# A hybrid decoder step on one core: the rates and keys stage appended to the input projection's block, its row products taken one by one, and the group norm's units ordered by head pair

## The chip, the cores and the metric

The kernel runs on one core of one Trainium2 chip. The metric is the device time of one execution in microseconds (us). Below, PE is TensorE, ACT is ScalarE, DVE is VectorE, POOL is GpSimd, and SP is SyncE, which issues most of the transfers.

## The reference, cut to what matters

One layer, for 1024 prompt tokens and 8 sequences of 8 sample tokens that share all weights (1088 tokens, width 1024):

```
x += 1/2 gate1 * SwiGLU1(mod(RMSNorm(x)))            # d_ff 2816
P  = mod(RMSNorm(x)) @ w_in                          # 1792 RWKV columns, 768 attention columns
z  = u + (u_shift - u) * mu_shift                    # r, k, v, zw, za, zg
decay = exp(-exp(-softplus(-(w0 + tanh(zw) @ w2)) - 0.5))
a  = sigmoid(a0 + za @ a2)
kk = k * k_k;  kk = kk * rsqrt(max(sum_head(kk * kk), 1e-24))
k  = k * (1 + (a - 1) * k_a)
S  = S * decay + (S @ -kk) (kk * a)^T + v k^T;  o = S @ r          # per head of 64, per token
o  = group_norm_head(o) * ln_x_w + ln_x_b + sum_head(r * k * r_k) * v
x += gate2 * [o * (sigmoid(zg) @ g2), windowed attention] @ w_out
x += 1/2 gate3 * SwiGLU2(mod(RMSNorm(x)));  y = RMSNorm(x)
```

The changed stage computes everything from `decay` to the new `k`, in a scaled form: the running product of the decays within a chunk of 64 tokens is an exponential of a running sum, and a, b, k and r are multiplied by it or by its inverse.

## The kernel before

The stages follow one another: `ffn` (first), `input_projection`, `rwkv_keys`, `rwkv_heads`, `ffn` (second). Each is one `Block` with a program for each engine, and at the end of a block all engines meet. Tensors lie with features on the partitions and tokens along the free axis. The 512 RWKV features are `PAIRS` = 4 pairs of heads m; the tokens are cut into `UTILES` of 384, 384 and 320, called t here; a unit i is one (t, m), with t outermost, `NU` = 12 of them.

**Input projection.** 20 column groups (`WIN_ORDER`), each in three token tiles (`TILES`) of 368, 368 and 352. PE does 24 matmuls for each into banks 0 to 2; ACT takes the result out (`evac`, L1694), DVE adds the previous token's share (`add_previous`, L1812 to L1823), and counts each in `u_free`. Attention work (banks 3 to 7) lies between the products. The last column group has the sums of the keys' squares (bank 5), their root on ACT (L1780) and the reciprocal on DVE (L1891), which leaves `kk_rows`: 8 rows for each t, at partition 32t. After the last product, PE turns the last tokens' columns in bank 7 (L1673), ACT copies them out (L1797), and SP writes them to memory.

**Seam.** Then comes `k.release(...)` (L227): it clears semaphores and lets all engines meet a second time. `rwkv_keys` and `rwkv_heads` have only the end of a block between them.

**Rates and keys (`rwkv_keys`).** PE: for each unit, two products of 64 rows (`lora`, L1987: decay and a, in the two halves of the rows) into banks 0, 1 and 5 in turn; each has its own wait and its own increment. After each of the first four units, `back(m)` spreads the norms of pair m over the heads: three products of 8 rows (L1913, one for each t, in rows 0, 32 and 64) into banks 2 to 4, with one wait and one increment. Then `modulation(0)` (four products of `w_ada`, L275, each on a 1 MB slab that SP loads into one of three buffers once the product three before it has been done), the `bonus` products of the units (L2006), and between them the second modulation and two transposes (L283). ACT: the sigmoids (`rates`, L2030 and L2032), `key_factors(t)` for all four pairs at once (L2038) after unit 3 and after unit 11, then per unit two exponentials (L2048, L2049) and, six units behind, the copy of the bonus (L2069). DVE: `head_rk` (L2121), a copy of the scan's keep row into bank 7 (L2124), the keys (L2095), the running sums (L2102), and per unit four operations of `scale` (L2113 to L2118). POOL: per t, four products b (L2149), then per pair the new k and the bonus factor (L2153, L2155).

**Heads and group norm (`rwkv_heads`).** The recurrence in chunks; at its end the group norm over 12 units `FINISH` of (t, m), here with t outermost and tiles of 384, 384 and 256 tokens. In its last loop PE does, per unit, `back(i)` (L2606: 8 rows at partition 32t, spread over the heads) and `gate(i - 1)` (L2615: 128 rows), with the sample sequences' work in between (`sample_state(m)`: L2570, L2572, L2575). DVE scales unit i (L2816), then gates unit i-2 (L2822), POOL adds the bonus (L2394), and ACT and POOL split the result for the output projection, which begins the second `ffn` (L476 to L478). `gate(i)` waits until DVE has gated unit i-2.

Of the kernel before, what the change touches and what calls it, by code (L numbers as in the profile page):

```python
# [24 lines left out]
ALU = mybir.AluOpType  # L25
# [3 lines left out]
P = 128  # L29
# [1343 lines left out]
N_QKV = 6  # L1373

# [5 lines left out]
NK = WINDOW + TSEQ  # L1380


def input_projection(k):
# [33 lines left out]
    bank_s, bank_t, bank_o = k.psum[3:5], k.psum[5:7], k.psum[7]  # L1417
    LAST = 2 * NA + 2
# [39 lines left out]
    with k.nc.Block() as block:  # L1458
        @block.sync
        def _(sp):  # L1460
# [27 lines left out]
            for n in range(4, NC):  # L1488
# [4 lines left out]
                if n == 8:  # L1493
# [8 lines left out]
                    for s in range(NSEQ):  # L1502
# [10 lines left out]
            k.gates.load(sp, 6, 0, 0)  # L1513
            sp.wait_ge(last_done, 1)
# [3 lines left out]
                         ).then_inc(k.shift_out, 16)  # L1518

        @block.gpsimd  # L1520
        def _(pool):
            norm.odd_lows(pool, 2)
            for n in range(2, NC):
                win.low(pool, n)
                if n == 2:
                    pool.wait_ge(mm_done, at(0, NT - 1))
                    for j in range(2):
                        pool.memset(rot[j][:], 0.0).then_inc(zeroed, 1)
                if n == N_QKV + 2:
                    pool.wait_ge(roped, 5)  # L1530
                    pool.tensor_copy(q_new[:].rearrange("p s (c t) -> p s c t", t=TSEQ),
                                     k.qkv[:, 0:4, NP_TOK:T].rearrange("p c (s t) -> p s c t", t=TSEQ)).then_inc(q_done, 1)

        @block.tensor
        def _(pe):
# [118 lines left out]

            def previous():
                pe.wait_ge(shift_in, 16)
                pe.transpose(k.psum[7][:, 0:NR], k.shift_rows[0:NR, :], k.c("ident")[0:NR, 0:NR]).then_inc(prev_mm, 1)
# [13 lines left out]
            pe.wait_ge(z_done, UC)  # L1671
            pe.wait_ge(o_done, NA)
            pe.transpose(k.psum[7][0:9 * UC, 0:P], k.last[:].rearrange("p s c -> p (s c)"), k.c("ident")).then_inc(last_mm, 1)  # L1673

        @block.scalar
        def _(act):
# [79 lines left out]
            def attention(s):  # L1756
# [21 lines left out]
                if s == LAST + 3:  # L1778
                    act.wait_ge(ss_done, 1)
                    act.activation(k.kk_rows[0:72, :], k.kk_rows[0:72, :], ACT.Sqrt).then_inc(root_done, 1)  # L1780

# [13 lines left out]
            act.activation(k.es[0], k.es[0], ACT.Sigmoid)  # L1795
            act.wait_ge(last_mm, 1)
            act.copy(k.last_rows[0:9 * UC, :], k.psum[7][0:9 * UC, 0:P]).then_inc(last_done, 1)  # L1797

        @block.vector
        def _(dve):  # L1800
# [78 lines left out]
            for n in range(NC):  # L1879
                if n >= N_QKV:  # L1880
                    for t in range(NT):
# [7 lines left out]
                        if s == LAST + 4:  # L1889
                            dve.wait_ge(root_done, 1)  # L1890
                            dve.reciprocal(k.kk_rows[0:72, :], k.kk_rows[0:72, :])  # L1891
# [4 lines left out]


UNITS = [(t, m) for t in range(len(UTILES)) for m in range(PAIRS)]
NU = len(UNITS)


def sums_to_rows(k, pe, bank, m, sq):

    for t, (a, n) in enumerate(UTILES):
        ins = pe.matmul(bank[32 * t:32 * t + 8, 0:n], k.c("to_rows")[:, 8 * m:8 * m + 8], sq[:, a:a + n],
                        start=(m == 0), stop=(m == PAIRS - 1))
    return ins


def row_to_heads(k, pe, out, m, t, rows):  # L1910

    r, n = slice(32 * t, 32 * t + 8), UTILES[t][1]
    return pe.matmul(out[:, 0:n], k.c("from_rows")[r, P * m:P * m + P], rows[r, 0:n], start=True, stop=True)  # L1913


def rows_to_heads(k, pe, banks, m, rows):

    for t in range(len(UTILES)):
        ins = row_to_heads(k, pe, banks[t], m, t, rows)
    return ins  # L1920


def rwkv_keys(k):

    d = k.dram
    C = float(np.exp(-0.5))
    k.bb = k.at("bb", R1_AT + PAIRS * TB, [P, PAIRS, T])  # L1930
    k.bon = k.at("bon", R1_AT, [P, PAIRS, T])
    log_d = k.at("log_d", R1_AT + 3 * PAIRS * TB, [P, PAIRS, T])
    keep, w2a2, ada = k.keep, k.w2a2, k.gates
    head_rk = k.at("head_rk", R2_AT + TB + 4 * RW, [P, PAIRS, P])
    turned = k.psum[5][:, 0:256]
    lora_mm, rates_done, back_mm, kk_done, kf_done = (
        k.sem(f"pr_{n}") for n in ("lora_mm", "rates_done", "back_mm", "kk_done", "kf_done"))
    sum_done, exp_done, b_done, bonus_in, bonus_mm, bonus_done, scaled = (
        k.sem(f"pr_{n}") for n in ("sum_done", "exp_done", "b_done", "bonus_in", "bonus_mm", "bonus_done", "scaled"))
    rk_done = k.sem("pr_rk_done")  # L1940

    KEEP_FROM = NP_TOK - TW_U
    KEEP0 = [0 if a < UTILES[-1][0] else a - KEEP_FROM for a, n in UTILES]
    NT_U = len(UTILES)

    def cut(tensor, m, t):
        a, n = UTILES[t]
        return tensor[:, m, a:a + n]

    def spans(t):  # L1950

        a, n = UTILES[t]
        out = [(0, min(a + n, NP_TOK) - a, HD)]
        if a + n > NP_TOK:
            out.append((NP_TOK - a, n, TSEQ))
        return out

    def lora_bank(n):
        return k.psum[(0, 1, 5)[n % 3]]

    def inv_bank(i):
        return k.psum[2 + i % 2][:, 0:UTILES[UNITS[i][0]][1]]

    def prd_bank(i):
        return k.psum[4 if i % 2 == 0 else 7][:, 0:UTILES[UNITS[i][0]][1]]

    def bonus_bank(i):
        return k.psum[i % 2][:, 0:UTILES[UNITS[i][0]][1]]

    with k.nc.Block() as block:  # L1970
        @block.sync
        def _(sp):
            for s in range(1, 8):
                if s >= 3:
                    sp.wait_ge(ada.used, s - 2)
                ada.load(sp, 6 + s // 4, s % 4, s % 3)
            sp.wait_ge(k.shift_out, 32)

        @block.tensor
        def _(pe):  # L1980
            def lora(i):
                t, m = UNITS[i]
                a, n = UTILES[t]
                for h, r in enumerate(HALVES):
                    if 2 * i + h >= 3:
                        pe.wait_ge(rates_done, 2 * i + h - 2)
                    pe.matmul(lora_bank(2 * i + h)[:, 0:n], w2a2[r, P * m:P * m + P], k.u[r, 12, a:a + n], start=True, stop=True  # L1987
                              ).then_inc(lora_mm, 1)

            def modulation(n):  # L1990
                if n:
                    pe.wait_ge(ada.rows, n)
                for s in range(4 * n, 4 * n + 4):
                    ada.product(pe, s % 4, s % 3, s // 3 + 1)
# [6 lines left out]
            def bonus(i):  # L2001
                t, m = UNITS[i]
                pe.wait_ge(bonus_in, i + 1)
                if i >= 2:
                    pe.wait_ge(bonus_done, i - 1)
                pe.matmul(bonus_bank(i), head_rk[:, m], cut(k.bon, m, t), start=True, stop=True).then_inc(bonus_mm, 1)  # L2006

            pe.wait_ge(k.lora_in, 32)
            for i in range(NU):
                lora(i)  # L2010
                if i < PAIRS:
                    back(i)
            pe.wait_ge(rates_done, 2 * NU)
            modulation(0)
            pe.wait_ge(rk_done, 1)
            for i in range(NU):
                bonus(i)
                if i == 1:
                    ada.turn(pe, 0, turned)
                    modulation(1)  # L2020
                if i == 7:
                    ada.turn(pe, 1, turned)

        @block.scalar
        def _(act):
            def rates(i):
                t, m = UNITS[i]
                n = UTILES[t][1]
                act.wait_ge(lora_mm, 2 * i + 1)
                act.activation(cut(log_d, m, t), lora_bank(2 * i)[:, 0:n], ACT.Sigmoid, bias=k.p2("rwkv_w0", m)).then_inc(rates_done, 1)  # L2030
                act.wait_ge(lora_mm, 2 * i + 2)
                act.activation(cut(k.bb, m, t), lora_bank(2 * i + 1)[:, 0:n], ACT.Sigmoid, bias=k.p2("rwkv_a0", m)  # L2032
                               ).then_inc(rates_done, 1)

            def key_factors(t):
                act.wait_ge(rates_done, 2 * PAIRS * (t + 1))
                for m in range(PAIRS):
                    act.activation(cut(k.bon, m, t), cut(k.bb, m, t), ACT.Identity, scale=k.p2("rwkv_k_a", m),  # L2038
                                   bias=k.one_ka[:, m:m + 1]).then_inc(kf_done, 1)

            def exps(i):
                t, m = UNITS[i]
                act.wait_ge(sum_done, NU if i == 1 else i + 1)
                if i >= 2:
                    act.wait_ge(scaled, i - 1)
                else:
                    act.wait_ge(kk_done, NU)
# [1038 lines left out]
```

## Time and profile before

| | |
|---|---|
| three runs | 2457.2, 2460.49, 2455.1 us; median 2457.2 |
| profiled execution | 2462.48 us, of which the span of the trace is 2460.4 |
| granted TensorE clock, mean | 0.978 |
| PE busy | 2367.4 us, 96% of the span |
| DVE, POOL, ACT busy | 1104.2, 537.9, 387.5 us |
| rates and keys | 1194.7 to 1251.5 us |
| group norm's last loop | 1498.9 to 1539.9 us |

Times of rows are in us from the start of the span. A timeline row has a start, a length, the engine, the line, the operation, its shapes and the number of instructions merged in it; a bracket tells how long the engine stood idle before it and what released it. An fp32 product is two MATMUL instructions. A granted clock of 1.00 is 2.4 GHz and 0.50 is 1.2 GHz.

### The profile page before, as it was taken

How to read it: one execution, taken by the hardware profiler on the slowest of the kernel's cores; microseconds unless marked ns; L12 is line 12 of the kernel's file. 1: busy time of each engine (PE TensorE's matmuls, PEld its weight loads, DVE VectorE, ACT ScalarE, POOL GpSimd, SP SyncE). 2: the span in 40 equal slices, each digit the busy share in tenths (PEclk: the TensorE clock that was granted, in tenths of full speed). 3: DMA queues.
4: the chain of work that ended last, by engine and by line, in shares of the span. 5: the costliest groups of instructions: out<-in, count | busy, mean ns of one | idle time of the engine just before them, and what ended most of it. 6: DMA issues, size and time to landing. Idle time of an engine off the chain costs nothing. (4 is left out here: it accounts for less than half of the span.)

```text
span 2460.4 us, 50589 instructions
## 1 busy us (share of the span) xinstructions
PE 2367.4 (96%) x21666; PEld 2247.0 (91%) x21666; DVE 1104.2 (45%) x2446; ACT 387.5 (16%) x890; POOL 537.9 (22%) x278
## 2 busy tenths in 40 slices
PE   5999999999999999999889899999999999999997
PEld 4999999999999989888468885999999999999997
DVE  4524443334444364434577664147334444433344
ACT  4100000000000232434521122131000000000003
POOL 2312121212212032111332133413212112121111
PEclk8999999999999999999799998999999999999999
DMA  9232221111011142100220002332111011111101
GB/s 338 86 103 84 87 86 52 50 36 51 17 51 51 49 111 59 35 26 30 98 66 5 4 13 63 107 103 69 45 41 50 18 51 51 51 51 34 51 9 73
DMA packets 160634, 151.22 MB, mean 61 GB/s; under 512 B 21488, under 2 KB 141985, under 8 KB 160088
## 3 DMA queue, kind: packets, MB, share of 16 engines
q1 hardware_dynamic: 159960, 146.75, 19.0%
q8 instruction: 119, 1.95, 0.3%
q10 hardware_dynamic: 144, 2.23, 0.2%
q14 instruction: 27, 0.22, 0.0%
q0 software_dynamic: 384, 0.07, 0.0%
HBM read 137.98 MB, written 11.34 MB: 61 GB/s over the span
## 5 line engine op out<-in xcount | busy, mean ns | idle before, releaser
L476 PE MATMUL bank<-hh,f_up_hi 128*128 128x368 f32 (+1 forms) x2112 | 693.4, 328 | 11.4 <-ACT hh L416 9.5
L478 PE MATMUL bank<-hh,f_up_lo 128*128 128x368 f32 (+1 forms) x2112 | 690.9, 327 | 0.0
L477 PE MATMUL bank<-hl,f_up_hi 128*128 128x368 f32 (+1 forms) x2112 | 690.2, 327 | 0.0
L1189 DVE TENSOR_TENSOR f_prod<-f_silu,bank 128x368 f32<-128x368 f32 x132 | 70.2, 532 | 767.4 <-PE bank L478 767.3
L476 PEld LDWEIGHTS bank<-hh,f_up_hi 128*128 128x128 f32 x2112 | 396.8, 188 | 17.7 <-issue 17.6
L477 PEld LDWEIGHTS bank<-hl,f_up_hi 128*128 128x128 f32 x2112 | 397.0, 188 | 0.0
L478 PEld LDWEIGHTS bank<-hh,f_up_lo 128*128 128x128 f32 x2112 | 396.9, 188 | 0.0
L491 DVE SCALAR_TENSOR_TENSOR x<-bank,mods,x 128x368 f32<-128x368 f32 (+1 forms) x544 | 306.2, 573 | 200.3 <-PE bank L478 188.1
L944 POOL TENSOR_TENSOR f_up_lo<-f_up_raw,f_up_hi 128x2048 fp32r<-128x2048 f32 x44 | 203.3, 4620 | 778.1 <-DVE f_up_hi L1176 778.1
L476 PE MATMUL bank<-f_a_hi,f_dn_hi 128*128 128x368 f32 (+1 forms) x1056 | 346.6, 328 | 0.8 <-DVE f_scratch L494 0.8
L478 PE MATMUL bank<-f_a_hi,f_dn_lo 128*128 128x368 f32 (+1 forms) x1056 | 345.3, 327 | 0.0
L477 PE MATMUL bank<-f_a_lo,f_dn_hi 128*128 128x368 f32 (+1 forms) x1056 | 344.8, 327 | 0.0
L1127 ACT ACTIVATE f_silu<-bank 128x368 f32<-128x368 f32 x132 | 62.4, 473 | 1442.1 <-PE bank L478 1442.1
L476 PEld LDWEIGHTS bank<-f_a_hi,f_dn_hi 128*128 128x128 f32 x1056 | 198.2, 188 | 1.7 <-DVE f_scratch L494 1.3
L477 PEld LDWEIGHTS bank<-f_a_lo,f_dn_hi 128*128 128x128 f32 x1056 | 198.3, 188 | 0.0
L478 PEld LDWEIGHTS bank<-f_a_hi,f_dn_lo 128*128 128x128 f32 x1056 | 198.2, 188 | 0.0
L949 POOL TENSOR_TENSOR f_dn_lo<-f_dn_raw,f_dn_hi 128x2048 fp32r<-128x2048 f32 x22 | 102.3, 4650 | 383.3 <-DVE f_dn_hi L1182 383.3
L476 PE MATMUL bank<-hh,w_in_hi 128*128 128x368 f32 (+1 forms) x480 | 163.7, 341 | 2.2 <-POOL hl L408 2.2
L477 PE MATMUL bank<-hl,w_in_hi 128*128 128x368 f32 (+1 forms) x480 | 159.1, 331 | 0.0
L478 PE MATMUL bank<-hh,w_in_lo 128*128 128x368 f32 (+1 forms) x480 | 158.9, 331 | 0.0
L476 PEld LDWEIGHTS bank<-hh,w_in_hi 128*128 128x128 f32 x480 | 91.9, 192 | 15.0 <-issue 14.7
L1362 POOL TENSOR_TENSOR w_in_lo<-w_in_raw,w_in_hi 128x1024 fp32r<-128x1024 f32 x18 | 47.1, 2614 | 223.0 <-DVE w_in_hi L1357 223.0
(377 smaller groups left out, 2814.7 us busy)
## 6 DMA issues: line engine op xcount, KB each, us to landing
f_up_raw<-in_ffn_w_gu SPq DMA_DIRECT2D x88, 512.0 KB, 5.0
f_dn_raw<-in_ffn_w_down SPq DMA_DIRECT2D x22, 1024.0 KB, 7.6
ada<-in_w_ada SPq DMA_DIRECT2D x12, 1024.0 KB, 16.2
late<-in_w_ada SPq DMA_DIRECT2D x12, 1024.0 KB, 4.9
w_in_raw<-in_w_in SPq DMA_DIRECT2D x16, 512.0 KB
gates<-in_w_ada SPq DMA_DIRECT2D x8, 1024.0 KB, 6.4
x_in<-in_x_prompt SPq DMA_DIRECT2D x8, 512.0 KB, 8.5
gate<-in_w_ada SPq DMA_DIRECT2D x4, 1024.0 KB, 5.1
```

What stands on the lines that cost most here:

```text
L476: pe.matmul(out, wh, rh, start=(n == 0), stop=False)
L477: pe.matmul(out, wh, rl, start=False, stop=False)
L478: ins = pe.matmul(out, wl, rh, start=False, stop=(n == last))
L491: ins = dve.scalar_tensor_tensor(x[:, a:a + np_], bank[:, 0:np_], gate[:, 0:1], x[:, a:a + np_], ALU.mult, ALU.add)
L944: pool.tensor_tensor(up_lo[j][:], up_raw[:], up_hi[j][:].bitcast(F32), ALU.subtract).then_inc(up_lo_done, 1)
L949: pool.tensor_tensor(dn_lo[:], dn_raw[:], dn_hi[:].bitcast(F32), ALU.subtract).then_inc(dn_lo_done, 1)
L1127: act.activation(silu[u % 2][:, 0:n], k.psum[2 * (u % 2)][:, 0:n], ACT.Silu).then_inc(gate_free, 1)
L1189: dve.tensor_tensor(prod[u % 2][:, 0:n], silu[u % 2][:, 0:n], k.psum[2 * (u % 2) + 1][:, 0:n], ALU.mult).then_inc(up_free, 1)
L1362: pool.tensor_tensor(lo[:], self.raw_of(n)[:], hi[:].bitcast(F32), ALU.subtract).then_inc(self.lo_done, 1)
```

## The change

`rwkv_keys` is no longer a block. It returns five functions, one for each engine, that `input_projection` calls at the end of its own programs, so that each engine goes on without meeting the others. What the meeting gave is now written as waits: `lora` waits for `u_free` (called `u_last`) and, for bank 5, for `ss_done`; the row products wait for the last `u_free`, for `max_done`, `t_done` and for a new semaphore `kk_ready` behind the reciprocal; DVE waits for `o_done` before it writes bank 7, for `win.lo_done` before `head_rk`; the modulation waits for `last_done`, as does the bonus.

- `back(m)` with three row products becomes twelve `back(q)`, each with its own wait and increment, through banks 2, 3, 4 and 6; they stand after units 1 to 5 in groups of 3, 2, 3, 2 and 2.
- `key_factors` is spread: from unit 4 on, ACT does one key factor after each unit's rates. The factors of the third t stay where they were.
- The transpose of the last tokens moves behind unit 7 and to bank 6; the sigmoid that brings in ACT's table moves up behind the root (L1780).
- DVE does all twelve keys before the first running sum, and `head_rk` after the last.
- SP issues the slabs 1 and 2 of the first modulation when the last product is done, ahead of the last tokens' transfers.
- `k.release` stands between this joint block and `rwkv_heads`.
- `FINISH` is ordered by pair: (0,3), (1,3), (0,2), (1,2), ... for the first eight units; the third t is as before. PE's last loop takes two units at a time: `back(2j)`, `back(2j+1)`, `gate(2j-1)`, `gate(2j)`.

```diff
+    BACK_BANKS = (2, 3, 4, 6)
+    BACK_AT = {1: (0, 1, 2), 2: (3, 4), 3: (5, 6, 7), 4: (8, 9), 5: (10, 11)}
...
-                    if 2 * i + h >= 3:
-                        pe.wait_ge(rates_done, 2 * i + h - 2)
+                n_before = 2 * i + h
+                if n_before >= 3:
+                    pe.wait_ge(rates_done, n_before - 2)
+                elif n_before == 2:
+                    pe.wait_ge(ss_done, 1)
+                else:
+                    pe.wait_ge(u_last, U_SLOTS - 2 + n_before)
...
-            def back(m):
-                if m >= 1:
-                    pe.wait_ge(kk_done, NT_U * m)
-                rows_to_heads(k, pe, k.psum[2:5], m, k.kk_rows).then_inc(back_mm, 1)
+        def back(q):
+            if q == 0:
+                pe.wait_ge(u_last, U_SLOTS)
+                pe.wait_ge(max_done, NA)
+                pe.wait_ge(kk_ready, 1)
+            elif q == 3:
+                pe.wait_ge(t_done, 2 * NA)
+            elif q >= len(BACK_BANKS):
+                pe.wait_ge(kk_done, q + 1 - len(BACK_BANKS))
+            m, t = divmod(q, NT_U)
+            row_to_heads(k, pe, back_bank(q), m, t, k.kk_rows).then_inc(back_mm, 1)
...
             for i in range(NU):
                 lora(i)
-                if i < PAIRS:
-                    back(i)
+            for q in BACK_AT.get(i, ()):
+                back(q)
+            if i == PAIRS + 3:
+                pe.wait_ge(kk_done, NU)
+                turn_last(pe)
...
             for i in range(PAIRS):
                 rates(i)
-            key_factors(0)
             for i in range(PAIRS, NU):
                 rates(i)
-            key_factors(1)
+            key_factors(i // PAIRS - 1, (i % PAIRS,))
+            if i == PAIRS + 4:
+                copy_last(act)
...
-FINISH = [(t, m) for t in range(3) for m in reversed(range(PAIRS))]
+FINISH = [(t, m) for m in reversed(range(PAIRS)) for t in range(2)] + [(2, m) for m in reversed(range(PAIRS))]
...
-            for i in range(FSAMPLE):
-                back(i)
-                if i >= 1:
-                    gate(i - 1)
+            for j in range(FSAMPLE // 2):
+                back(2 * j)
+                back(2 * j + 1)
+                if j:
+                    gate(2 * j - 1)
+                gate(2 * j)
...
         input_projection(k)
-        k.release(keep=(k.cache_out, k.shift_out, k.lora_in, k.keep_in, *k.gates.sems))
-        rwkv_keys(k)
+        k.release(keep=(k.cache_out,))
         rwkv_heads(k)
```

## Rows read from the trace of the kernel before

**Rows 1.** The page: busy time of each engine, share of the span, instructions.
```profile
PE 2367.4 (96%) x21666; PEld 2247.0 (91%) x21666; DVE 1104.2 (45%) x2446; ACT 387.5 (16%) x890; POOL 537.9 (22%) x278
```

**Rows 2.** Busy time by stretch: PE, PEld, DVE, ACT, POOL, clock, DMA share, GB/s.
```profile
1190.00:1252.00 62.00, 46.17 (x245) 21.01 (x249) 42.17 (x90) 38.91 (x87) 33.92 (x38) 0.72 0.34 120
1252.00:1456.00 204.00, 181.53 (x7005) 173.62 (x6996) 142.92 (x334) 28.73 (x62) 31.94 (x40) 1.00 0.05 11
1456.00:1542.00 86.00, 82.44 (x1092) 50.03 (x1087) 41.61 (x69) 28.49 (x54) 43.27 (x46) 0.85 0.18 53
```

**Rows 3.** Timeline of PE, from the last input product to the heads.
```profile
1189.39 0.32 PE L478 MATMUL bank<-hh,w_in_lo 128*128 128x352 f32 x1
...
1194.74 1.65 PE L1987 MATMUL bank<-au,w2a 64*128 64x384 f32 x4 [2.92 <-PEq L230]
1196.32 1.65 PE L1913 MATMUL bank<-kk_rows,const 8*128 8x384 f32 x6
1197.90 1.65 PE L1987 MATMUL bank<-au,w2a 64*128 64x384 f32 x4
...
1208.01 11.31 PE L1987 MATMUL bank<-au,w2a 64*128 64x384 f32 x32
1219.94 2.80 PE L275 MATMUL bank<-gates,cT 128*32 128x256 f32 x48 [0.62 <-ACT bb L2032]
...
1239.73 1.36 PE L275 MATMUL bank<-gates,cT 128*32 128x256 f32 x16 [2.65 <-DMA gates<-in_w_ada]
1241.03 4.45 PE L2006 MATMUL bank<-bon,head_rk 128*128 128x384 f32 x8
...
1251.58 0.33 PE L2234 MATMUL bank<-au,bb 64*64 64x128 f32 x2 [0.77 <-PEq L1970]
```

**Rows 4.** Timeline of ACT in the same stretch.
```profile
1191.85 0.27 ACT L1797 COPY last_rows<-bank 126x128 f32<-126x128 f32 x1
1196.40 0.58 ACT L2030 ACTIVATE log_d<-bank,par 128x384 f32<-128x384 f32 x1 [4.28 <-PE bank L1987]
1196.87 0.57 ACT L2032 ACTIVATE bb<-bank,par 128x384 f32<-128x384 f32 x1
...
1207.40 2.50 ACT L2038 ACTIVATE bon<-bb,rest,par 128x384 f32<-128x384 f32 x4
...
1250.85 0.42 ACT L2069 COPY bon<-bank 128x320 f32<-128x320 f32 x1 [0.21 <-PE bank L2006]
```

**Rows 5.** Timeline of DVE in the same stretch.
```profile
1190.89 0.27 DVE L1816 SCALAR_TENSOR_TENSOR au<-bank,par,au 128x56 f32<-128x56 f32 x1
...
1224.53 0.55 DVE L2113 SCALAR_TENSOR_TENSOR au<-au,bank 128x378 f32<-128x378 f32 x1 [4.37 <-POOL bb L2149]
...
1249.51 0.23 DVE L307 SCALAR_TENSOR_TENSOR mods<-mods,par 128x72 f32<-128x72 f32 x1
```

**Rows 6.** Timeline of POOL in the same stretch.
```profile
1208.28 3.87 POOL L2149 TENSOR_TENSOR bb<-bb,au 128x384 f32<-128x384 f32 x4 [43.59 <-ACT bon L2038]
...
1242.71 0.86 POOL L2155 TENSOR_TENSOR bon<-au 128x320 f32<-128x320 f32 x1
```

**Rows 7.** Two single microseconds around the rise of the clock, columns as in rows 2.
```profile
1215.00:1216.00 1.00, 1.00 (x4) 0.95 (x4) 0.96 (x1) 0.99 (x2) 0.86 (x2) 0.50 0.00 0
...
1217.00:1218.00 1.00, 0.98 (x6) 0.66 (x5) 0.51 (x1) 0.94 (x4) 0.86 (x2) 1.00 0.00 0
```

**Rows 8.** Timeline of PE in the group norm's last loop.
```profile
1498.92 1.64 PE L2606 MATMUL bank<-gn_rows,const 8*128 8x384 f32 x2
...
1512.03 0.91 PE L2615 MATMUL bank<-au,g 128*128 128x384 f32 x2
1512.88 0.91 PE L2606 MATMUL bank<-gn_rows,const 8*128 8x384 f32 x2
```

**Rows 9.** Timeline of DVE in the same loop.
```profile
1512.14 0.61 DVE L2816 SCALAR_TENSOR_TENSOR au<-au,par,bank 128x384 f32<-128x384 f32 x1 [3.40 <-PE bank L2606]
1512.67 0.55 DVE L2822 TENSOR_TENSOR au<-au,bank 128x384 f32<-128x384 f32 x1
```

More of the change, by code:

```diff
@@ L1380, with sums_to_rows, row_to_heads @@
 NK = WINDOW + TSEQ
+UNITS = [(t, m) for t in range(len(UTILES)) for m in range(PAIRS)]
+NU = len(UNITS)
+def sums_to_rows(k, pe, bank, m, sq):
+    for t, (a, n) in enumerate(UTILES):
+        ins = pe.matmul(bank[32 * t:32 * t + 8, 0:n], k.c("to_rows")[:, 8 * m:8 * m + 8], sq[:, a:a + n],
+                        start=(m == 0), stop=(m == PAIRS - 1))
+    return ins
+def row_to_heads(k, pe, out, m, t, rows):
+    r, n = slice(32 * t, 32 * t + 8), UTILES[t][1]
+    return pe.matmul(out[:, 0:n], k.c("from_rows")[r, P * m:P * m + P], rows[r, 0:n], start=True, stop=True)
@@ L1417, in input_projection @@
     bank_s, bank_t, bank_o = k.psum[3:5], k.psum[5:7], k.psum[7]
+    kk_ready = k.sem("kk_ready")
+    keys = rwkv_keys(k, win, u_free, max_done, ss_done, t_done, o_done, kk_ready, last_done)
+    keys_sync, keys_tensor, keys_scalar, keys_vector, keys_gpsimd = keys
     LAST = 2 * NA + 2
@@ L1513, in _ @@
             k.gates.load(sp, 6, 0, 0)
+            sp.wait_ge(mm_done, at(NC - 1, NT - 1))
+            k.gates.load(sp, 6, 1, 1)
+            k.gates.load(sp, 6, 2, 2)
             sp.wait_ge(last_done, 1)
@@ L1653, in attention, with turn_last @@
                         key_sums(2 * (s - LAST - 1) + m)
+            def turn_last(pe):
+                pe.wait_ge(z_done, UC)
+                pe.wait_ge(t_done, 2 * NA)
+                pe.transpose(bank_t[1][0:9 * UC, 0:P], k.last[:].rearrange("p s c -> p (s c)"), k.c("ident")).then_inc(last_mm, 1)
             def previous():
@@ L1670, in _ @@
                         attention(slot(n, t))
-            pe.wait_ge(z_done, UC)
-            pe.wait_ge(o_done, NA)
-            pe.transpose(k.psum[7][0:9 * UC, 0:P], k.last[:].rearrange("p s c -> p (s c)"), k.c("ident")).then_inc(last_mm, 1)
+            keys_tensor(pe, turn_last)
         @block.scalar
@@ L1780, in attention, with copy_last @@
                     act.activation(k.kk_rows[0:72, :], k.kk_rows[0:72, :], ACT.Sqrt).then_inc(root_done, 1)
+                    act.activation(k.es[0], k.es[0], ACT.Sigmoid)
+            def copy_last(act):
+                act.wait_ge(last_mm, 1)
+                act.copy(k.last_rows[0:9 * UC, :], bank_t[1][0:9 * UC, 0:P]).then_inc(last_done, 1)
             norm.roots(act, 2)
@@ L1794, in _ @@
                         attention(slot(n, t))
-            act.activation(k.es[0], k.es[0], ACT.Sigmoid)
-            act.wait_ge(last_mm, 1)
-            act.copy(k.last_rows[0:9 * UC, :], k.psum[7][0:9 * UC, 0:P]).then_inc(last_done, 1)
+            keys_scalar(act, copy_last)
         @block.vector
@@ L1895, in _ @@
                     rope(n - 1)
[L1898 to L1913, printed above, removed]
@@ L2729, in _ @@
             sample_o_end()
[L2730 to L2734 removed]
+            for j in range(FSAMPLE // 2):
[4 more added lines that the diff above has]
+                gate(2 * j)
+                if j == 0:
                     sample_mean()
[L2736 removed]
+                if j == 2:
                     sample_sums()
[L2738 removed]
+                if j == 3:
                     sample_back()
[L2740 to L2741 removed]
+                if j < PAIRS:
+                    sample_state(j)
             gate(FSAMPLE - 1)
```

401 lines of the change are left out of this document (200 added, 201 removed).

## The prediction

> **What bounds the kernel now.** The page's first part comes first: PE is busy 2367.4 of 2460.4 us, and no other engine reaches half [rows 1]. So the time is PE's, and a change can win only where PE is not doing full work. The busy time by stretch shows where that is: from 1190 to 1252 us PE is busy 46.2 of 62 us and at a mean clock of 0.72, so both idle and slow; in the group norm's stretch it is busy nearly always, but at 0.85 [rows 2]. These are the two places that the diff touches. Nothing else in PE's order changes, so what either stage saves or costs moves all that follows it, one for one.
>
> In the first place the timelines are read engine by engine. PE's last input product ends at 1189.71, its first rates product starts at 1194.74, the last ends at 1219.32, and the heads start at 1251.58 [rows 3]. Which chain ties 1219.32 to 1251.58? PE starts the modulation at 1219.94; its slabs are loaded one after another, each into a buffer that an earlier product must have left, and the last of the eight arrives at 1239.73, where PE had waited for the transfer. Behind that product in PE's order stand ten of the twelve bonus products, which start at 1241.03, alternate with ACT's exponentials and end with ACT's copy at 1251.27 [rows 3, 4]. DVE is done at 1249.74, POOL at 1243.57 [rows 5, 6]. So the end of the stage hangs on the start of the modulation, and that on the end of the rates products.
>
> **Part 1, the seam in front.** The products for unit 0 and the first of unit 1 need no result of the last tile, so PE goes on at 1189.71 in place of 1194.74. The second of unit 1 needs the first rate from ACT. ACT is free at about 1190.4, since its table load has moved up; that load, 1.3 us by the idle stretch it then fills behind the root, lies in front of the evacuation of the last group's second tile, which only feeds DVE, and DVE's reciprocal ends as ACT takes out the third tile: I cost it at nothing, and at 1.3 us if DVE turns out late. With a rate of 0.58 [rows 4] this product starts at 1191.1. The first three row products need DVE's last add, which ends at 1191.16 [rows 5]. Together they end at about 1192.4 (lower bound 1191.9, if they run alone at full clock; upper 1193.0, if they fall to the half clock).
>
> **Part 2, rates and row products.** Before, the stretch from 1194.74 to 1219.32 held twelve pairs of rates products and four groups of row products. A pair and a group take 1.58 each at the half clock of that stretch (1196.32 - 1194.74, 1197.90 - 1196.32) [rows 3]. One row product alone takes 1.57 at that clock too (1.64 with its tail), and three in one group 1.65 [rows 3, 8]: products in different rows run side by side, and a group costs what one of them costs. Do they still when each has its own wait and increment? The trace shows no single row products with waits of their own, but it shows the pairs of rates products, which have them and still take 1.65 for two. So I take five groups at 1.58, one of them already counted in part 1. The bounds: 0 more if all share, and 7 x 1.57 = 11.0 us more if none of the seven that ride along does. Their waits for DVE (a bank is free after the key four products before it) are one or two groups old when PE comes to them. What is left after 1192.4 is ten pairs and four groups: 24.58 - 2 x 1.58 = 21.4 us, and 0.4 for the transpose that has moved in: 1214.2. That is 5.1 us earlier than 1219.32.
>
> The Trainium skill ("TensorE: Matmul & The Clock Gate", section "The cost: per-tile semaphore tail") says that increments of packed products queue up at some 26 ns each. By it, an estimate, twelve increments in place of four add 8 x 26 ns = 0.2 us; the sum does without it.
>
> **Part 3, what follows from it.** ACT now does eight key factors between the rates: 0.62 each (2.50 / 4) beside 0.94 for a unit's two rates (2 x 0.47) [rows 4], so 1.56 a unit, as much as PE's pair at half clock: just covered, and it is what would bind if PE were faster. POOL begins its stream when the fourth factor is there. Before, it ran without a pause from 1208.28 to 1243.57 [rows 6]. After, the fourth factor comes with unit 7 at about 1209.3, when three of the four b are done, so POOL is only 1.9 us ahead and ends at 1241.7: still before the end of the chain. DVE's twelve keys, twelve sums and `head_rk` are done by about 1217.4, and the scales, which took 25.2 us with their waits (1224.53 to 1249.74) [rows 5], end before 1245. So the chain of slabs stays the last, 5.1 us earlier: ACT's last copy at 1246.2. The two slabs that SP now issues at 1189.7 were never the late ones (they have until 1214); I cost that at nothing, with or without it. The last tokens' transfers move behind ACT's copy at unit 8, hidden under 30 us of the stage. **Stage: -5.1.**
>
> **Part 4, the release moves back.** From ACT's copy (end 1192.12) to PE's start at 1194.74 the release and the two meetings take 2.6 us; from ACT's last copy (1251.27) to the heads at 1251.58 one meeting takes 0.3 [rows 3, 4]. The release now stands at the second place, the cheap meeting at the first is gone. The 2.6 contains SP's two last transfers (about 0.8), which won't be there. So +1.5, between +1.2 and +2.3.
>
> **Part 5, the group norm.** In PE's last loop a row product takes 0.84 and a gate 0.85 at full clock (1512.03 to 1512.88 and on) [rows 8], and PE never waits. The first eight units now alternate between rows 0 and 32, so two row products run for the price of one: 4 x 0.84 = 3.4 us. But `gate(2j)` now needs DVE's gating of unit 2j-2, which stands behind the scaling of unit 2j: 0.61 + 0.55 less overlap, and about 0.1 for each handover, 1.25 us after the row product [rows 9]; PE has only `gate(2j-1)`, 0.85, to do meanwhile. Three times about 0.35, so -3.4 + 1.1 = **-2.3**. Who waits behind that gate is `sample_state`, and nobody else. The last four units share the same rows and gain nothing. The sums of the early units run side by side too, but they wait for ACT's squares: nothing. Bounds: -3.4, and 0 if the slower part of the clock (0.50 in the rows at 1498.92 [rows 8]) grows by as much as is saved.
>
> **The sum.** -5.1 + 1.5 - 2.3 = -5.9. On the profiled execution's own 2462.5 us that is 2456.6. That execution lies 5.3 above the median of 2457.2; the same difference on the median gives **2451.3**.
>
> **The rivals.**
> *The clock stays full in the rates.* Before, the clock was still 0.50 at 1215 and 1.00 only at 1217, with PE busy all the time since 1194.74 [rows 3, 7]; ahead of that the engine had been idle for most of 5 us. After, that gap is below 1 us. If the clock stays at 2.4 GHz, ACT binds: from 1190.4, eight units at 0.94, four at 0.84, eight factors at 0.62 and a copy, 16.1 us, to 1206.5; the modulation starts 13.2 us earlier, its chain ends at 1238.1, after POOL (about 1234) and DVE (about 1236). The sum is -13.2 + 1.5 - 2.3 = -14.0: 2443.2. Against it: in the rates of before, PE was never idle and stayed at 1.2 GHz for over 20 us with products of 64 and of 8 rows; they don't seem to count as full work. The Trainium skill, "TensorE: Matmul & The Clock Gate" (Part 1), holds that the array is slow by default and sustained matmul activity gives it the full clock; by that rule PE, never idle for long now, would be at full clock here. The trace agrees only in part, with 0.50 at 1215 under a PE that is busy all the time [rows 7]. Chance 0.17.
> *The loop of the group norm gives nothing.* The clock there falls and rises with the mix of products, and two products at once leave PE more idle rows or more waits; -5.1 + 1.5 = -3.6: 2453.6. Chance 0.22.
> *The heads start at half clock.* The release leaves PE idle for nearly 2 us right before the heads, after a thin stretch, where before it was 0.8. Heads are 89% PE [rows 2]; each microsecond at 1.2 GHz costs up to 0.5. Below 12 us it only eats the gain, 2457 at most; from about 22 us on the kernel is slower by more than 0.2%. Against it: at 1.00 these products held the full clock for 204 us. Chance 0.07.
> *The single row products don't overlap.* Then part 2 costs 11.0 more and the group norm gives nothing and adds no wait: -5.1 + 11.0 + 1.5 = +7.4: 2464.6, slower. It decides from the fourth of the seven on (4 x 1.57 > 5.9), and shows as slower by 0.2% only with all seven. Against it: the pairs of rates products. Chance 0.06.
>
> **How the numbers follow.** The likeliest case has what is left, 0.48, with a range of its own from -9.5 to -2.5 (the clock rising earlier or later by one change, the bounds of parts 1, 4 and 5). All cases together: 2443 holds the full-clock case, 2458.5 all but the last. What a measurement of this kernel tells from no change is about 0.2%, or 4.9 us. Below 2452.3 lie two thirds of the likeliest case, nearly all of the full-clock one and a fifth of the third: 0.32 + 0.16 + 0.05 = 0.53. Above 2462.1: the last rival and a rest of the fourth, 0.08. Between, 0.39.
>
> **What would show it.** PE's first rates product right after the last input product, with no gap of 5 us; rates products ending near 1214; L275 starting then, and its last slab near 1234.6; the heads' first product near 1248; groups of row products with 1.6 us for two or three; in the last loop pairs of 384-column row products at about 0.9 us for two. The prediction is wrong if the clock in the rates is 1.00, if the row products stand in line, if POOL's or DVE's stream and not the slabs ends the stage, or if the heads begin at 0.50.

## The result and the profile after

The changed kernel takes **2446.6 us** (median of 7 runs, 2442.4 to 2449.5) against 2457.2 for the kernel before (7 runs on the same chip). The ratio is 0.995, with an interval of [0.9939, 0.9961], so it saves between 9.6 and 15.0 us; the ratio itself stands for 12.3, and the medians differ by 10.6. The forecast was 2451.3, a gain of 5.9. The direction was right. The mechanism named for the first place was wrong in its clock: what came there was the rival to which the forecast gave 0.17. The profiled execution took 2446.64 us, with a span of 2444.9. It lies on the median, whereas the profiled execution of before lay 5.3 above its own.

The page's busy line, against [rows 1]: PE is busy for 15.8 us less, with the same 21666 instructions. So the products themselves became shorter, not only the gaps between them.

```profile
PE 2351.6 (96%) x21666; PEld 2237.9 (92%) x21666; DVE 1105.4 (45%) x2446; ACT 386.2 (16%) x890; POOL 537.1 (22%) x278
```

Busy time by stretch, columns as in [rows 2]. The first stretch is 10 us shorter, and its mean clock is 0.90 where it was 0.72. The heads are unchanged.

```profile
1190.00:1242.00 52.00, 38.05 (x225) 15.70 (x223) 43.37 (x90) 36.23 (x82) 33.56 (x36) 0.90 0.39 143
1242.00:1446.00 204.00, 181.90 (x7015) 174.00 (x7016) 143.21 (x334) 28.74 (x62) 32.55 (x41) 1.00 0.05 11
1446.00:1530.00 84.00, 76.61 (x1095) 49.32 (x1092) 41.00 (x69) 28.82 (x55) 44.28 (x47) 0.88 0.21 60
```

Timeline of PE from the last input product to the heads, against [rows 3]:

```profile
1188.78 0.32 PE L478 MATMUL bank<-hh,w_in_lo 128*128 128x352 f32 x1
1189.03 2.49 PE L1480 MATMUL bank<-au,w2a 64*128 64x384 f32 x8
1191.44 0.91 PE L1399 MATMUL bank<-kk_rows,const 8*128 8x384 f32 x6
1192.29 0.92 PE L1480 MATMUL bank<-au,w2a 64*128 64x384 f32 x4
1193.13 0.91 PE L1399 MATMUL bank<-kk_rows,const 8*128 8x384 f32 x4
...
1206.68 0.80 PE L1480 MATMUL bank<-au,w2a 64*128 64x320 f32 x2 [0.21 <-ACT log_d L1534]
1208.52 2.80 PE L275 MATMUL bank<-gates,cT 128*32 128x256 f32 x48 [1.04 <-ACT bb L1536]
...
1228.14 1.94 PE L275 MATMUL bank<-gates,cT 128*32 128x256 f32 x16 [3.38 <-DMA gates<-in_w_ada]
1230.01 4.50 PE L1508 MATMUL bank<-bon,head_rk 128*128 128x384 f32 x8
...
1242.08 0.33 PE L2271 MATMUL bank<-au,bb 64*64 64x128 f32 x2 [2.29 <-PEq L230]
```

There is no gap at 1189, and a pair of rates products or a group of row products takes 0.85 from start to start, where before it took 1.58. That is the full clock, as the window over the middle of them shows (columns as in [rows 2]):

```profile
1198.00:1202.00 4.00, 3.97 (x16) 1.68 (x15) 3.28 (x6) 3.92 (x9) 2.18 (x3) 1.00 0.00 0
```

The rates products end at 1207.48, the modulation starts at 1208.52 (before: 1219.94) and the heads start at 1242.08 (before: 1251.58). The last input product ends at 1189.10, before at 1189.71, so 0.6 us of each of these differences was gained ahead of the changed stage.

Timelines of ACT, DVE and POOL in the same stretch, against [rows 4 to 6]:

```profile
1184.63 1.28 ACT L2074 ACT_TABLE_LOAD   x1
...
1197.57 0.70 ACT L1542 ACTIVATE bon<-bb,rest,par 128x384 f32<-128x384 f32 x1
...
1239.83 0.43 ACT L1573 COPY bon<-bank 128x320 f32<-128x320 f32 x1 [0.21 <-PE bank L1508]
```

```profile
1209.80 3.04 DVE L1635 TENSOR_SCALAR head_rk<-const,par 128x128 f32<-128x128 f32 x4
1212.76 0.54 DVE L1618 SCALAR_TENSOR_TENSOR au<-au,bank 128x378 f32<-128x378 f32 x1
...
1238.49 0.23 DVE L307 SCALAR_TENSOR_TENSOR mods<-mods,par 128x72 f32<-128x72 f32 x1
```

```profile
1198.44 1.00 POOL L1654 TENSOR_TENSOR bb<-bb,au 128x384 f32<-128x384 f32 x1 [34.36 <-DVE au L1600]
...
1234.77 0.87 POOL L1660 TENSOR_TENSOR bon<-au 128x320 f32<-128x320 f32 x1
```

ACT's last copy ends the stage at 1240.26, DVE is done at 1238.72 and POOL at 1235.64. The slabs' chain still binds, and the release behind it takes 1.8 us, as forecast.

Timeline of PE in the group norm's last loop, against [rows 8]:

```profile
1495.24 0.91 PE L2643 MATMUL bank<-gn_rows,const 8*128 8x384 f32 x4
1496.09 0.91 PE L2652 MATMUL bank<-au,g 128*128 128x384 f32 x2
1497.32 0.91 PE L2652 MATMUL bank<-au,g 128*128 128x384 f32 x2 [0.32 <-DVE au L2861]
```

Two row products run in 0.85. Of the two gates behind them, the second waits 0.32 for DVE's gating. The same wait comes three times (1497.32, 1503.04, 1509.30).

### The profile page after: what moved, and what is told of

It is laid out like the page before. It is cut to its first block and busy times, and to the rows that moved or that the text cites. A ratio compares the mean times of both kernels' runs of the same rounds, so it can differ in the third digit from the quotient of the medians.

```text
span 2444.9 us, 50581 instructions
## 1 busy us (share of the span) xinstructions
PE 2351.6 (96%) x21666; PEld 2237.9 (92%) x21666; DVE 1105.4 (45%) x2446; ACT 386.2 (16%) x890; POOL 537.1 (22%) x278
## 3 DMA queue, kind: packets, MB, share of 16 engines
q1 hardware_dynamic: 159960, 146.75, 19.1%
## 5 line engine op out<-in xcount | busy, mean ns | idle before, releaser
L476 PE MATMUL bank<-hh,f_up_hi 128*128 128x368 f32 (+1 forms) x2112 | 693.3, 328 | 11.8 <-ACT hh L416 9.5
```

What stands on the lines that cost most here:

```text
L476: pe.matmul(out, wh, rh, start=(n == 0), stop=False)
```

## The experiments

All medians stand beside the kernel before on the same chip. A gain in us that stands behind a ratio is worked out from that ratio; it can differ from the difference of the two medians by one or two us. The two parts of the change were first taken alone.

**The stage alone.** The changed kernel with the group norm of before:

```diff
-FINISH = [(t, m) for m in reversed(range(PAIRS)) for t in range(2)] + [(2, m) for m in reversed(range(PAIRS))]
+FINISH = [(t, m) for t in range(3) for m in reversed(range(PAIRS))]
...
-            for j in range(FSAMPLE // 2):
-                back(2 * j)
-                back(2 * j + 1)
-                if j:
-                    gate(2 * j - 1)
-                gate(2 * j)
+            for i in range(FSAMPLE):
+                back(i)
+                if i >= 1:
+                    gate(i - 1)
```

> The joint block alone, group norm in the old order. My reading of the trace after: the seam and the rates hold most of the gain, because PE no longer idles before the rates and they run at 2.4 GHz. Expected -8 us against before (about 2449), with L1480-type rates products ending within 19 us of the last input product and a clock of 1.00 there. Rival: the clock has nothing to do with it and the append brings only what was forecast, -3.6 us (2453.6).

Measured: 2449.4 against 2459.8, ratio 0.9964 [0.9951, 0.9977], or -8.9 us. In its trace the rates products end 18.4 us after the last input product, as in the changed kernel. The expectation of -8 us held.

**The group norm alone.** The same edit the other way round, on the kernel before.

> The group norm's order alone, on the kernel before. Expected -2.5 us (2454.7): four pairs of row products that share their time, less three waits of 0.3 us, plus 1 us in the sums. The forecast had -2.3. Rival: it gives as much as the trace after shows between the row products and the output projection (-5), then it would be 2452.

Measured: 2452.8, ratio 0.9971 [0.9959, 0.9983], or -7.1 us. That is three times my -2.3. The two parts alone add up to -16.0, more than the -12.3 of the whole. The intervals are wide enough to allow that; the runs are repeated below.

**The gap in front of the rates.** Is it the idle stretch that decides the clock? The first kernel is the changed one with nine ACT copies ahead of the first rate, and PE's first rates product waits for them. The second kernel has the same copies and the same wait, but PE does seven products (fourteen passes) of 128 rows in the time in which it would stand idle.

```diff
+            pe.wait_ge(held, 1)
...
+        for j in range(9):
+            ins = act.copy(k.bon[:, j % 4, 352 * (j // 4):352 * (j // 4) + 352], k.u[:, 4, 0:352])
+        ins.then_inc(held, 1)
```

```diff
+            pe.wait_ge(u_last, U_SLOTS - 2)
+            pe.wait_ge(max_done, NA)
+            for _ in range(7):
+                pe.matmul(k.psum[3][:, 0:384], k.c("ident"), k.u[:, 12, 0:384], start=True, stop=True)
```

> The kernel after, but ACT does nine more copies (352 columns each, about 3.9 us) before its first rate, and PE stands idle until they are done; no result is changed. If an idle stretch before the rates is what puts PE at 1.2 GHz for the whole of them, the clock is 0.50 there and the time is up by 4 + about 7 us (2457). If the mix of products sets the clock and not the idle stretch, the clock stays 1.00 and the time is up by 4 us (2450.6).

> The same as gap_idle, with seven products of 128 rows and 384 columns on PE in the time in which it stood idle there (results not used). Both theories: the clock stays 1.00 and the time is up by 4 us against after (2450.6). If it falls to 0.50 here as well, the delay itself and not the idle PE matters, for example the place of the rates in time.

Measured: 2461.0 with the idle gap, ratio 1.0006 [0.9997, 1.0015], and 2453.2 with the filled one, ratio 0.997 [0.9958, 0.9982]. PE's timeline of the kernel with the idle gap, and the window over its rates:

```profile
1188.28 0.32 PE L478 MATMUL bank<-hh,w_in_lo 128*128 128x352 f32 x1
1192.82 3.96 PE L1481 MATMUL bank<-au,w2a 64*128 64x384 f32 x8 [4.22 <-ACT bon L1578]
1196.70 1.65 PE L1399 MATMUL bank<-kk_rows,const 8*128 8x384 f32 x6
...
1215.22 6.54 PE L1481 MATMUL bank<-au,w2a 64*128 64x320 f32 x16
```

```profile
1193.00:1221.00 28.00, 28.00 (x72) 11.40 (x73) 15.37 (x23) 15.15 (x30) 7.42 (x8) 0.50 0.10 40
```

And PE's timeline of the kernel with the filled gap:

```profile
1190.40 4.68 PE L1514 MATMUL bank<-au,const 128*128 128x384 f32 x14
1195.01 2.49 PE L1481 MATMUL bank<-au,w2a 64*128 64x384 f32 x8
1197.43 0.92 PE L1399 MATMUL bank<-kk_rows,const 8*128 8x384 f32 x6
```

PE comes to its first rates product equally late in both, 4.2 and 4.5 us after the last input product. But after 4.22 us of idling it runs 28 us at a clock of 0.50, though never idle, and after products it runs at full clock. From first to last, the rates products take 28.9 us in the one (1192.82 to 1221.76) and 19.1 in the other (1195.01 to 1214.10). The medians differ by 7.8 us, as expected, and every run shows the difference: the mean granted clock of a whole execution is 0.978 to 0.981 in all eleven runs with the idle gap and 0.982 to 0.986 in all six with the filled one. So the rates run slowly after an idle stretch of this size and fast when full-height products stand in its place. Whether any work would do in its place, or only products of 128 rows, was not separated.

**The gap filled in the kernel before.** If the gap is all that matters, filling products should do in the kernel before what the joined block does. Three of them stand ahead of the wait for DVE's last add and two behind the transpose.

```diff
+            pe.wait_ge(max_done, NA)
+            for _ in range(3):
+                pe.matmul(k.psum[3][:, 0:384], k.c("ident"), k.u[:, 12, 0:384], start=True, stop=True)
...
+            for _ in range(2):
+                pe.matmul(k.psum[3][:, 0:384], k.c("ident"), k.u[:, 12, 0:384], start=True, stop=True)
```

> The kernel before, with three products of 128 rows and 384 columns on PE ahead of its wait for the last tile and two behind the transpose (results not used), so that PE idles about 1.7 us in one piece ahead of the rates and not 1.8 and 2.9. If the idle stretch alone is what put the rates at 1.2 GHz, they run at 2.4 GHz now and are bound by ACT: about -7 us against before (2452), as much as the append gained beyond its forecast and more. If it needs the append as well (rates that follow the products without a pause), nothing changes, or it is up by the 0.3 us by which PE may come late to the meeting.

Measured: 2454.1 against 2455.6, ratio 0.9993 [0.9984, 1.0002]. A miss. PE's timeline and windows:

```profile
1195.12 0.92 PE L1992 MATMUL bank<-au,w2a 64*128 64x384 f32 x4 [1.70 <-PEq L230]
1195.97 0.91 PE L1918 MATMUL bank<-kk_rows,const 8*128 8x384 f32 x6
1196.81 1.54 PE L1992 MATMUL bank<-au,w2a 64*128 64x384 f32 x4
1198.60 1.65 PE L1918 MATMUL bank<-kk_rows,const 8*128 8x384 f32 x6 [0.25 <-DVE au L2100]
```

```profile
1197.00:1211.00 14.00, 13.48 (x41) 5.26 (x40) 11.16 (x18) 7.36 (x15) 3.81 (x4) 0.51 0.34 136
1211.00:1218.00 7.00, 6.36 (x35) 3.36 (x36) 5.59 (x7) 6.94 (x15) 6.57 (x8) 1.00 0.00 0
```

The rates begin at full clock; the clock falls at 1197 and rises again at 1211. The rates end 26.7 us after the last input product, where before it was 29.6. The wait for the last slab takes most of that back: its product starts at 1239.06, 0.7 earlier than in [rows 3]. The 1.70 us of the release was left idle here. In the joined block, which has no such gap, the clock stayed full. That this rest of a gap is the reason is not shown: one execution without any gap, below, also lost the clock.

**Key factors, and two ways of ending the stage sooner.** There are three variants of the changed kernel. One has the key factors in groups of four again. One has the first three slab products moved up behind the last three units of rates. The third has, on top of that, `head_rk` computed in DVE's wait ahead of the keys.

```diff
+        key_factors(0)
...
-            key_factors(i // PAIRS - 1, (i % PAIRS,))
...
+        key_factors(1)
```

```diff
+            if i >= NU - 3:
+                early(i - NU + 3)
```

> The kernel after, with the key factors of the first t in one piece behind unit 3 and those of the second behind unit 11, as before. The slabs of the modulation end the stage in the trace after, so the order of the factors should be worth nothing either way: within 1 us of after (2446.6). Rival: POOL or ACT binds and the spread was worth something; then it is 2 us or more slower.

> The kernel after, with the first three products of the modulation behind units 9, 10 and 11 in place of behind all rates, so that their buffers come free about 2.5 us earlier. If only the transfers set the end of the stage, it ends up to 2.5 us earlier (2444). If the fifth product's wait for DVE (its rows are copied behind the third scale) sets when the last slab is asked for, it gives about nothing, or costs up to 1 us where the products stand in ACT's way.

> early_slabs, and DVE makes head_rk while it waits for the first row products, where POOL is idle. In after it took 3.04 us there against 0.87 before. Expected: 0.87 again, the scales 1.5 to 2 us earlier, and with both waits eased the stage ends 2 to 3 us earlier than in after (2444). Rival: the copy of the rows is not late for any slab, and the end moves by less than 1 us.

Measured, against 2455.6: 2446.9 with the factors grouped, ratio 0.9961 [0.9949, 0.9974]; 2443.3 with early slabs, 0.9952 [0.9939, 0.9966]; 2443.2 with `head_rk` as well, 0.9953 [0.994, 0.9966]. What spreading the factors is worth can't be told from these medians. The trace of the kernel with grouped factors showed something else. PE's timeline, and the window behind it:

```profile
1193.08 0.92 PE L1480 MATMUL bank<-au,w2a 64*128 64x384 f32 x4
1193.92 1.12 PE L1399 MATMUL bank<-kk_rows,const 8*128 8x384 f32 x4
1194.98 1.65 PE L1480 MATMUL bank<-au,w2a 64*128 64x384 f32 x4
```

```profile
1196.00:1215.00 19.00, 18.70 (x49) 7.87 (x47) 13.02 (x20) 11.38 (x23) 11.70 (x12) 0.50 0.04 14
```

There is no gap ahead of the rates, and yet the clock falls inside the row products at 1194.7. The edit can't be the cause: ACT does its first key factor at 1197.60, and up to the fall this kernel and the changed one do the same. In this execution the rates end 24.8 us after the last input product and the heads start 59.1 after it, close to my likeliest case. So the joined block allows the full clock; it does not guarantee it. Of the eight profiled executions with the joined block and no added gap this is the only one. The runs without a profile hint at a few more: the stage alone had one of 2457.8 us in the first set and one of 2459.0 in the repeat, both with a mean clock of 0.979, where its others show 0.981 to 0.986. The mean of a whole execution doesn't tell where the clock was low, so this stays a hint.

With early slabs the last slab's product starts at 1225.94 (in the changed kernel at 1228.14), which is 2.3 us earlier when counted from the last input product. Timelines of PE without and with the moved `head_rk`:

```profile
1235.35 2.77 PE L1512 MATMUL bank<-bon,head_rk 128*128 128x320 f32 x8
1240.41 0.33 PE L2277 MATMUL bank<-au,bb 64*64 64x128 f32 x2 [2.29 <-PEq L230]
```

```profile
1235.62 4.27 PE L1512 MATMUL bank<-bon,head_rk 128*128 128x320 f32 x8
1242.18 0.33 PE L2277 MATMUL bank<-au,bb 64*64 64x128 f32 x2 [2.29 <-PEq L230]
```

The second comes to its last slab 0.9 us sooner (1225.02), but 0.7 of that lies ahead of the stage, so the moved `head_rk` brings 0.2 there. It then starts the heads 2.4 us later, counted from the last input product. Of this 1.5 us is that the last eight passes run at half clock (4.27 in place of 2.77). The rest lies between the last slab and these passes.

**The same again, on one chip.** To see whether the parts add, and whether the clock repeats, three of these kernels and the changed one were run side by side.

> The changed kernel once more, as the yardstick of the other three on the same chip. It stood 10.6 us below the kernel before (0.995). If the full clock in the joint block is what the block gives whenever nothing empties TensorE's queue, the rates' products end some 18 to 19 us after the last input product again. If it is a matter of chance from one execution to the next, as the one execution with grouped key factors suggests, some profiled executions of these four kernels show it at half by 1196, and the rates end 7 us later in them.

> The appended stage alone, with the group norm as before. Alone it stood 8.9 us below the kernel before, the group norm alone 7.1 us, both together 10.6 us: these don't add up. Theory A, the two parts are additive and the earlier two medians were each a few us off: here the appended stage gives 6 to 8 us and the difference to the changed kernel is 3 to 5 us. Theory B, the group norm's part is worth less behind the appended stage: 9 us again, and a difference of under 2.5 us.

> The group norm's order alone, on the kernel before. Theory A (additive): 3 to 5 us below the kernel before. Theory B (worth more by itself than behind the appended stage): 7 us again. My forecast of this part was 2.3 us, which would be a ratio of 0.9991.

> The changed kernel with the first three modulation products issued after the last three rate units. In its profiled execution the heads began 1.7 us earlier than in the changed kernel's. If that is the kernel's and not the execution's, its median stands 1.5 to 3.5 us below that of the changed kernel on this chip; if not, within 1 us.

Measured, against 2460.8:

| kernel | median us | ratio, interval |
|---|---|---|
| changed kernel | 2449.8 | 0.9952 [0.9936, 0.9967] |
| stage alone | 2451.8 | 0.9964 [0.9953, 0.9974] |
| group norm alone | 2455.7 | 0.9982 [0.9971, 0.9992] |
| early slabs | 2448.3 | 0.9958 [0.9941, 0.9976] |

The changed kernel repeats, and so does the stage alone. So the stage alone came as theory B had it (-8.9 again, and 2.0 between its median and that of the changed kernel), and the group norm alone as theory A had it (-4.4). The two alone now sum to -13.3 against -11.8 for both together, so they add up within the intervals. The intervals of the group norm's -7.1 and -4.4 overlap, and neither is shown to be off. How much the group norm is worth behind the new stage these medians don't settle. They don't tell early slabs from the changed kernel either.

The traces say more, since each profiled execution can be cut at the same instructions. All times are in us: from the last input product's end to the last rates product's end, to the heads' start, and from the first row product of the last loop to the first output product.

| kernel (one execution) | rates end | heads start | last loop |
|---|---|---|---|
| before | 29.6 | 61.9 | 43.1 |
| before, fillers | 26.7 | 61.5 | 41.0 |
| group norm alone, twice | 29.6; 29.6 | 65.5; 62.7 | 40.5; 37.1 |
| stage alone, twice | 18.4; 19.0 | 52.8; 53.8 | 40.7; 40.1 |
| changed, twice | 18.4; 18.4 | 53.0; 54.5 | 39.0; 36.9 |
| factors grouped | 24.8 | 59.1 | 36.9 |
| early slabs, twice | 19.3; 19.3 | 51.2; 51.2 | 37.0; 36.8 |
| early slabs, `head_rk` | 19.3 | 53.7 | 36.9 |
| idle gap; filled gap | 33.2; 23.5 | 67.6; 57.4 | 36.9; 40.6 |

The mean of the stage is 63.4 in the three executions with the old stage and no filler, and 53.5 in the four with the new stage: -9.8. Four executions of the old loop average 41.2 and ten of the new one 37.9: -3.4. Together that is -13.2, inside the interval of the ratio. The stretch between the two, in which only the order of the sums differs, varies by itself: from the heads' start to the last loop it takes 243.7 to 250.4 us over all fourteen. So does the old stage, with 61.9, 65.5 and 62.7 us in three executions, though their rates end at the same 29.6.

## Why the forecast was half right

The direction and the nearness of 2451.3 owe something to luck: most of the gain came for a reason that the forecast held unlikely, and the time that it gave to that rival, 2443.2, lies nearer to the measured 2446.6. The forecast's likeliest case had a range of its own from -9.5 to -2.5, and the measured -10.6 to -12.3 lies outside it. That the measured time lies inside the whole range, from 2443 to 2458.5, is due to the full-clock rival that the range had to hold. The forecast itself had called a clock of 1.00 in the rates a sign of being wrong.

**Part 1** held. PE goes on behind the last input product, and the first group of row products ends at 1192.35, by the forecast at 1192.4. Counted from the last input product that is 3.3 us against 2.7, at the upper bound; the times of 1192.35 and 1192.4 agree because the last input product ended 0.6 earlier here.

**Part 2 failed in its premise.** It priced a group at 1.58, the half clock that [rows 3] show, and set the end at 1214.2, 24.5 us after the last input product's end. The count was right: groups of two or three row products with waits of their own still cost one. The price was 0.85, and the rates ended 18.4 us after the last input product. I had seen that PE ran without a pause for 20 us at the half clock before and concluded that such thin products hold it there. The kernels with the idle and the filled gap show the other reading: in these two the products kept the clock that they found, for most of the block. Before, they found the half clock, after nearly 5 us with little to do. What makes the chip grant one level or the other stays open: the fillers in the kernel before, and the grouped-factors execution, lost the full clock under the same kinds of product. The full clock was the first rival, at 0.17. Its sum of -13.2 for the stage was 2.4 to 2.8 too large: counted from the last input product, the modulation starts 10.8 earlier and ACT's last copy ends 10.4 earlier. ACT doesn't bind from the start: up to unit 4 it still waits 0.64 to 1.10 for PE, and only from unit 6 on are the units 1.4 to 1.6 apart. The grouped-factors execution shows that the premise could have held: there the clock fell and the rates ended 24.8 us after the last input product.

**Part 3.** Its conclusion held, and its times moved with the clock. The slabs' chain ends last; DVE is done 1.5 us ahead of it and POOL 4.6. What the order of DVE cost was not in it: `head_rk` took 3.04 us in place of 0.87, now that POOL was running beside it. That the slabs' chain hid this fits the moved `head_rk`, whose median is the same as that of early slabs without it (2443.2 against 2443.3).

**Part 4** held: 1.8 us from ACT's last copy to the heads, against 0.3 before, so +1.5. `[2.29 <-PEq L230]` is its mark. Taking the release away was not tried.

**Part 5 was mis-sized.** The last loop gave -3.4 (41.2 to 37.9), not -2.3. The term that was mis-sized is "the last four units gain nothing". Below are windows over units 0 to 7 and over the last four, of the stage alone (old loop) and of the group norm alone (new loop), each in its repeat, where both loops start at full clock:

```profile
1494.80:1521.60 26.80, 26.80 (x219) 13.43 (x217) 10.55 (x18) 7.81 (x15) 14.97 (x14) 1.00 0.19 41
1521.60:1531.70 10.10, 10.10 (x19) 4.44 (x19) 5.77 (x12) 2.31 (x6) 6.97 (x9) 0.52 0.00 0
```

```profile
1498.90:1523.90 25.00, 24.03 (x219) 12.53 (x217) 10.29 (x18) 6.51 (x13) 14.92 (x14) 0.99 0.15 33
1523.90:1532.20 8.30, 5.93 (x20) 3.09 (x19) 5.50 (x12) 3.45 (x8) 6.28 (x8) 0.88 0.15 32
```

The first eight give 1.9 us. That is near the forecast: 3.4 from the paired row products, less three waits that cost 0.4 each. The last four give 1.8 more, and not because they overlap: PE is idle for 2.4 of 8.3 us in them, but the clock is 0.88 in place of 0.52. The output projection's first product then waits 0.7 longer. What makes the clock fall later in the new order is not settled. The rest of the spread is clock too. The three longest of the new loops begin at half clock (row products of 1.65, as in [rows 8]), and all the others at full clock or soon after. Among loops that begin so, the three of the old order average 40.6 and the seven of the new 36.9, so the gain is not an effect of where the loops happened to begin. The sums, which I had costed at nothing, show little: PE is busy with them for 7.8, 6.1, 6.1 and 7.8 us in four executions of the old order and for 6.2, 6.3, 7.1 and 7.0 in four of the new.

**The other rivals.** The single row products do overlap. The loop of the group norm did give something. The heads at half clock, at 0.07, did come, in small. In two executions, the repeats of the changed kernel and of early slabs, they start at it for 3 us. The first of these:

```profile
1244.59 0.48 PE L2271 MATMUL bank<-au,bb 64*64 64x128 f32 x2 [2.29 <-PEq L230]
```

In five more (both of the stage alone, grouped factors, the moved `head_rk`, the idle gap) the clock falls within 1.4 us of the heads' start and stays at 0.50 for about 3.4 us. So seven of the ten executions with the release in front of the heads show it, and none of the four with the old stage; the changed kernel's profile above happens to be one of the three without. Each costs at most half of its stretch, 1.7 us, and what it costs in the medians was not measured.

## What to carry to other kernels

When a stretch of thin products (few rows) runs at the half clock, that is no proof that such products always run at it. Look at what PE did just before, and if it idled for some us, price the stretch at both levels. When two programs are joined so that PE never stops between them, the gap can be the smaller part of the gain. Here it was 5 of the 11 us by which the rates end earlier, and the clock in the stretch behind it gave the other 6. A full clock won like this was lost in one of eight profiled executions. So compare several of them, cut at the same instructions, before you put a difference of a few us down to an edit.

## What was not expected of the hardware

Four DVE instructions that multiply a 128x128 tile by one column (`head_rk`) take 0.87 us where POOL is idle: so it was before, and again in the variant that moved them to 1190.15. Beside POOL's stream they took 3.0 us. In the changed kernel the first takes 273 ns and the median is 980 ns, which is the 1.00 of one POOL instruction. The Trainium skill ("SBUF — State Buffer", section "Who interferes with whom") says that a `tensor_scalar` may run in a mode that shares a port pair with GpSimd, and that one of the two then waits for the other's whole instruction. The trace agrees: the median of the four is 980 ns. The scales of DVE of 384 columns, which read a bank, take 0.54 to 0.55 in the same stretch.

With PE busy nearly all the time and the same kinds of product, the granted clock was 0.50 for 28 us after an idle stretch of 4.22 us (the kernel with the idle gap), and 1.00 from 1190 to 1207 without one (the changed kernel). The Trainium skill's rule, cited in the prediction's first rival, that sustained activity brings the full clock, is borne out only for the second.
